# The output projection of a hybrid layer by seven half-size products, and the order in which its weight places are freed

## The reference

```python
mixed = jax.nn.sigmoid(gate_a) * attn_branch + jax.nn.sigmoid(gate_s) * ssm_branch
x = x + mixed @ w_out[i]                      # 256x1024 by 1024x1024, float32
x = x + moe_swiglu(rmsnorm(x, g_ffn[i]), w_router[i], ...)   # top 4 of 32 experts
x = x + sigmoid(rmsnorm(x) @ w_ple_gate) * rmsnorm(p[i] @ w_ple_proj, g_ple_post)
```

## Time and profile before

| | |
|---|---|
| median of three runs | 1183.19 us (1183.05 to 1185.23) |
| the profiled execution | 1185.14 us, its span 1183.4 us |
| granted TensorE clock, mean | 0.992 of full |
| TensorE busy | 1126.7 us, 95% |
| VectorE, ScalarE, GpSimd busy | 372.6, 172.9, 117.6 us |
| DMA moved | 441.16 MB, mean 373 GB/s |
| TensorE in the chain that ended last | 85% |

### The profile page before, as it was taken

One profiled execution on the slowest core, in us unless ns is written; L12 is line 12 of the kernel. 1 busy time (PEld: TensorE's weight loads), 2 busy tenths in 40 slices (PEclk: granted clock), 3 DMA queues, 4 the chain that ended last, 5 costly groups with the idle time before them and its releaser, 6 DMA issues.

```text
span 1183.4 us, 15750 instructions
## 1 busy us (share of the span) xinstructions
PE 1126.7 (95%) x6562; PEld 504.8 (43%) x6562; DVE 372.6 (31%) x831; ACT 172.9 (15%) x262; POOL 117.6 (10%) x151
## 2 busy tenths in 40 slices
PE   7999999999999999999999999999999998999998
PEld 4588887633333333333323333333333333333344
DVE  6547853342222223222222222232222232222222
ACT  2262010510000000000211111111111111111121
POOL 2995650100000000000000000000000000000000
PEclk9999999999999999999979999999999999999999
DMA  9932348699999999999999999999999999999980
GB/s 304 346 116 72 142 165 323 231 415 416 420 430 433 428 432 434 426 433 434 425 394 417 432 434 431 426 435 432 426 436 433 425 435 433 426 435 425 426 347 36
DMA packets 38950, 441.16 MB, mean 373 GB/s; under 512 B 9604, under 2 KB 10176, under 8 KB 22400
## 3 DMA queue, kind: packets, MB, share of 16 engines
q1 hardware_dynamic: 35760, 436.75, 87.9%
q0 software_dynamic: 752, 2.36, 0.6%
q10 hardware_dynamic: 2400, 1.49, 0.4%
HBM read 439.54 MB, written 1.05 MB: 372 GB/s over the span
## 4 chain that ended last, share of the span: by engine, by line
PE 85%; DVE 6%; DMA 6%; ACT 2%; issue 1%; SPq 0%; DVEq 0%
PE bank L1568 35%; PE bank L1624 18%; PE bank L1258 7%; DMA ring<-in_w_up_dram 6%; PE bank L1642 5%; PE bank L1273 3%; PE bank L1463 2%; PE bank L1746 2%; PE bank L1418 2%; PE bank L1606 2%; DVE arena L1098 2%; DVE arena L1102 2%; DVE arena L1096 2%; PE bank L1429 2%; ACT arena L729 1%
## 5 line engine op out<-in xcount | busy, mean ns | idle before, releaser
L1568 PE MATMUL bank<-ring,arena 128*64 128x512 f32 x2048 | 450.7, 597 | 3.5 <-DMA ring<-in_w_up_dram 3.5
L1568 PEld LDWEIGHTS bank<-ring,arena 128*64 128x64 f32 x2048 | 144.2, 137 | 304.4 <-issue 298.1
L1624 PE MATMUL bank<-ring,arena 128*64 128x512 f32 x1024 | 228.5, 599 | 15.8 <-ACT arena L729 14.7
L1120 DVE TENSOR_TENSOR arena<-arena,bank 128x512 f32<-128x512 f32 x128 | 79.8, 682 | 294.8 <-PE bank L1642 294.6
L1624 PEld LDWEIGHTS bank<-ring,arena 128*64 128x64 f32 x1024 | 72.2, 137 | 151.4 <-issue 134.3
L1094 DVE TENSOR_SCALAR arena<-bank 128x512 f32<-128x512 f32 x32 | 22.1, 691 | 344.7 <-PE bank L1568 344.7
L727 ACT ACTIVATE arena<-arena 128x512 f32<-128x512 f32 x32 | 20.2, 630 | 466.3 <-DVE arena L1094 466.3
L1258 PE MATMUL bank<-arena,ring 128*128 128x256 f32 x384 | 86.4, 382 | 0.0
L1258 PEld LDWEIGHTS bank<-arena,ring 128*128 128x128 f32 x384 | 71.8, 190 | 12.7 <-issue 3.5
L1642 PE MATMUL bank<-arena 64*128 64x512 f32 x256 | 68.9, 624 | 0.0
L1542 PEld LDWEIGHTS bank<-arena 128*128 128x128 bf16 x1488 | 45.1, 98 | 25.2 <-issue 25.2
(11 more groups left out here) (250 smaller groups left out, 736.9 us busy)
## 6 DMA issues: line engine op xcount, KB each, us to landing
ring<-in_w_up_dram SPq DMA_DIRECT2D x45, 4096.0 KB, 24.7
ring<-in_w_down_dram SPq DMA_DIRECT2D x27, 4096.0 KB, 27.6
ring<-in_w_up_dram SPq DMA_DIRECT2D x36, 2048.0 KB, 23.5
ring<-in_w_down_dram SPq DMA_DIRECT2D x9, 2048.0 KB, 13.0
ring<-in_w_in_dram SPq DMA_DIRECT2D x7, 2048.0 KB, 16.2
ring<-in_w_glu_dram SPq DMA_DIRECT2D x2, 2048.0 KB, 8.2
ring<-in_w_out_dram SPq DMA_DIRECT2D x2, 2048.0 KB, 7.7
ring<-in_w_up_dram SPq DMA_DIRECT2D x4, 1024.0 KB, 32.4
```

The source lines that it names most:

```text
L1120: dve.tensor_tensor(part, part, bank[at][:, :], ALU.add).then_inc(m["sc_add"], 1)
L1568: last = pe.matmul(bank[UG + w][HALF * h:HALF * (h + 1), :].rearrange("p (m j) -> p m j", j=4), XS[:, k, :], columns[:, h, :, :], start=Fa ...
L1624: last = pe.matmul(bank[YB][HALF * c:HALF * (c + 1), :], ACTT[:, j, HALF * h:HALF * (h + 1)], piece[:, j, 512 * c:512 * (c + 1)], start=(h ...
```

## The change

The matrices are split in halves of the inner dimension and of both outer ones: for tokens early/late block t, inner half j, column half c. Four full products become seven products of four steps each. Sums of the right-hand quarters (`W_SUM`) are made by GpSimd, sums of the left-hand quarters (`M_SUM`) by VectorE. outa and outc accumulate several products in one bank, and VectorE adds the bank to a quarter of X2 after each (`prod_full`, `prod_read`). The seventh product is out3 and out4, in quarters, over columns 0 to 511 of block 1 (they were 512 to 1023).

```diff
+        H2T = area(A_X, DT, SEQ)
+        OUT_W = [[ring[:, PLACE * at:PLACE * (at + 1)].rearrange("p (j a n) -> p j a n", j=2, a=4)[:, j] for j in range(2)]
+                 for at in (6, 7)]
+        W_SUM = [area(A_Q, 4, 512), area(A_Q + 2048, 4, 512), OUT_W[1][0], area(A_BT, 4, 512)]
+        M_SUM = [area(A_GATE + 2048 + at, 4, P) for at in (0, 512, 1536, 1024)]
...
-        LAST = FIRST + (E - 1 - FIRST) // PERIOD * PERIOD
+        LAST = FIRST + 8 * PERIOD
...
+            return FIRST <= n <= LAST and spot(n, c) < PLACES - 1
+
+        HALVES = {(E - 2, 3): "late_0", (E - 1, 3): "late_1", (E - 1, 5): "late_2"}
...
-            for i in range(PLACES):
+            for i in (0, 1, 2, 3, 4, 5, 6, 8, 7):
                 at = spot(0, i)
-                if at in held:
+                if at == TURN["out", 0][0]:
+                    wait_full(sp, "outb")
+                    sp.wait_ge(S["w_sum"], 4)
+                elif at == TURN["out", 1][0]:
+                    wait_full(sp, "outa")
+                elif at in held:
                     wait_full(sp, held[at])
                 elif at == PLACES - 1:
-                    wait_full(sp, "lg1")
+                    sp.wait_ge(S["prod_full"], 3)
+                    sp.wait_ge(S["w_sum"], 4)
                 load_rows(at, expert_source(i // PER_EXPERT, i % PER_EXPERT))
...
-                pool.dma_start(BDOWN[rows, :], b_down[0, :, 512 * (g % 2):512 * (g % 2 + 1)]).then_inc(S["down_bias_in"], 16)
-            pool.dma_start(GPOST, g_ple_post[0:1, :].broadcast_to([P, D])).then_inc(S["post_in"], 16)
-            pool.wait_ge(S["mixed_set"], DT)
...
+            pool.tensor_tensor(W_SUM[0], OUT_W[1][0], OUT_W[0][0], ALU.subtract).then_inc(S["w_sum"], 1)
+            pool.wait_ge(S["w_sum"], 1)
+            pool.tensor_tensor(W_SUM[1], OUT_W[1][1], W_SUM[0], ALU.subtract).then_inc(S["w_sum"], 1)
+            pool.tensor_tensor(W_SUM[2], OUT_W[1][1], OUT_W[1][0], ALU.subtract).then_inc(S["w_sum"], 1)
+            pool.wait_ge(S["w_sum"], 3)
+            pool.tensor_tensor(W_SUM[3], OUT_W[0][1], W_SUM[1], ALU.subtract).then_inc(S["w_sum"], 1)
...
+            wait_full(pool, "lg1")
+            pool.dma_start(WPP, w_ple_proj[0].rearrange("(k p) n -> p k n", p=P)).then_inc(S["ple_in"], 16)
...
+            pool.dma_start(PIN, p[0, 0].rearrange("(t p) n -> p t n", p=P)).then_inc(S["ple_in"], 16)
...
+            pool.dma_start(GPOST, g_ple_post[0:1, :].broadcast_to([P, D])).then_inc(S["post_in"], 16)
...
-            act.dma_start(WPP, w_ple_proj[0].rearrange("(k p) n -> p k n", p=P)).then_inc(S["ple_in"], 16)
-            act.dma_start(PIN, p[0, 0].rearrange("(t p) n -> p t n", p=P)).then_inc(S["ple_in"], 16)
...
-
-            def squared(t, job, cols, to):
-                released(act, job)
+            act.activation(TABLE, ident[:, 0:1], ACT.Sqrt)
+
+            def squared(t, cols, to):
                 act.activation(JUNK[:, cols], X2[:, t, cols], ACT.Square,
                                accum_out=SSQ[:, to:to + 1]).then_inc(S["x2_sq"], 1)
 
...
-            released(act, "out0")
-            squared(0, "out1", slice(0, D), 2)
+            released(act, "outb")
+            squared(0, slice(0, 512), 4)
+            released(act, "outc")
+            squared(0, slice(512, D), 2)
             normal(0)
+            wait_full(act, "outc")
             cast(0, 0)
-            squared(1, "out2", slice(0, 512), 3)
+            act.wait_ge(S["prod_read"], 4)
+            squared(1, slice(512, D), 3)
+            released(act, "out3")
+            squared(1, slice(0, 256), 6)
             cast(0, 1)
-            squared(1, "out3", slice(512, 768), 6)
             cast(0, 2)
-            squared(1, "out4", slice(768, D), 7)
+            released(act, "out4")
+            squared(1, slice(256, 512), 7)
             normal(1)
             cast(1, 0)
...
+            early = [GATE[:, 0:4, P * t:P * (t + 1)] for t in range(TB)]
+            late = [GATE[:, 4:DT, P * t:P * (t + 1)] for t in range(TB)]
+            dve.tensor_tensor(M_SUM[0], early[1], late[1], ALU.add).then_inc(S["m_sum"], 1)
+            dve.wait_ge(S["m_sum"], 1)
+            dve.tensor_tensor(M_SUM[1], M_SUM[0], early[0], ALU.subtract).then_inc(S["m_sum"], 1)
+            dve.tensor_tensor(M_SUM[2], early[0], early[1], ALU.subtract).then_inc(S["m_sum"], 1)
+            dve.wait_ge(S["m_sum"], 2)
+            dve.tensor_tensor(M_SUM[3], late[0], M_SUM[1], ALU.subtract).then_inc(S["m_sum"], 1)
...
+            def add_product(t, c, job, full_by=None):
+
+                if full_by is None:
+                    wait_full(dve, job)
+                else:
+                    dve.wait_ge(S["prod_full"], full_by)
+                part = X2[:, t, 512 * c:512 * (c + 1)]
+                return dve.tensor_tensor(part, part, ps(job)[:, :], ALU.add)
+
+            add_product(0, 0, "outa", 1).then_inc(S["prod_read"], 1)
+            dve.wait_ge(S["prod_read"], 1)
+            release(add_product(0, 0, "outb"), "outb")
+            add_product(1, 1, "outc", 2).then_inc(S["prod_read"], 1)
+            add_product(0, 1, "outa", 3).then_inc(S["prod_read"], 1)
+            dve.wait_ge(S["prod_read"], 3)
+            release(add_product(0, 1, "outc"), "outc")
             dve.wait_ge(S["router_in"], 16 * 3)
             dve.tensor_tensor(WR, WR, spread(GROUT, E), ALU.mult).then_inc(S["router_set"], 1)
             dve.wait_ge(S["x2_sq"], 1)
-            mean_plus_eps(SSQ[:, 2:3], D).then_inc(S["x2_ms"], 1)
+            ts(SSQ[:, 4:5], SSQ[:, 4:5], D * EPS, None, ALU.add)
+            dve.wait_ge(S["x2_sq"], 2)
+            dve.tensor_scalar(SSQ[:, 2:3], SSQ[:, 2:3], SSQ[:, 4:5], 1.0 / D, ALU.add, ALU.mult).then_inc(S["x2_ms"], 1)
             dve.wait_ge(S["x2_root"], 1)
             dve.reciprocal(RSTD[:, 2:3], RSTD[:, 2:3]).then_inc(S["x2_normal"], 1)
-            add_output("out2", 1, slice(0, 512))
+            add_product(1, 1, "outa").then_inc(S["prod_read"], 1)
+            release(add_product(1, 0, "outa"), "outa")
             turned("xt0", 0, 0, 4)
             turned("xt1", 0, 4, 4)
-            add_output("out3", 1, slice(512, 768))
-            dve.wait_ge(S["x2_sq"], 3)
+            released(dve, "outa")
+            add_output("out3", 1, slice(0, 256))
+            dve.wait_ge(S["x2_sq"], 4)
             ts(SSQ[:, 6:7], SSQ[:, 6:7], SSQ[:, 3:4], D * EPS, ALU.add, ALU.add)
             dve.wait_ge(S["x2_normal"], 1)
             choose(0)
-            turned("xt2", 1, 0, 4)
-            turned("xt3", 1, 4, 2)
+            turned("xt2", 1, 4, 4)
+            turned("xt3", 1, 0, 2)
             ranked(0).then_inc(S["sel_first_set"], 1)
-            add_output("out4", 1, slice(768, D))
-            turned("xt4", 1, 6, 2)
-            dve.wait_ge(S["x2_sq"], 4)
+            add_output("out4", 1, slice(256, 512))
+            turned("xt4", 1, 2, 2)
+            dve.wait_ge(S["x2_sq"], 5)
             dve.tensor_scalar(SSQ[:, 3:4], SSQ[:, 7:8], SSQ[:, 6:7], 1.0 / D, ALU.add, ALU.mult).then_inc(S["x2_ms"], 1)
             dve.wait_ge(S["x2_root"], 2)
...
+            def product(job, of, w, ks=range(4), start=False, stop=True, cols=slice(0, 512)):
+
+                b = ps(job)[:, 0:cols.stop - cols.start]
                 for k in ks:
-                    last = pe.matmul(b[:, 0:SEQ], GATE[:, k, P:2 * P], weight(("out", 1), DT)[:, k, cols],
-                                     start=(k == 0), stop=(k == DT - 1))
-                if ks[-1] == DT - 1:
-                    done(last, job)
+                    last = pe.matmul(b, of[:, k, :], w[:, k, cols], start=start and k == 0, stop=stop and k == 3,
+                                     skip_group_check=True)
+                return last
+
+            def quarter(j, t):
+                return GATE[:, 4 * j:4 * (j + 1), P * t:P * (t + 1)]
...
-            output(0)
-            output(1)
-            output(2)
-            released(pe, "out0")
-            released(pe, "out1")
+            take("outa")
+            arrive(("out", 0))
+            pe.wait_ge(S["mixed_set"], 4)
+            product("outa", quarter(0, 0), OUT_W[0][0], start=True).then_inc(S["prod_full"], 1)
+            take("outb")
+            pe.wait_ge(S["mixed_set"], DT)
+            done(product("outb", quarter(1, 0), OUT_W[0][1], start=True), "outb")
+            take("outc")
+            pe.wait_ge(S["w_sum"], 2)
+            pe.wait_ge(S["m_sum"], 2)
+            product("outc", M_SUM[0], W_SUM[0], start=True).then_inc(S["prod_full"], 1)
+            pe.wait_ge(S["prod_read"], 1)
+            product("outa", M_SUM[1], W_SUM[1]).then_inc(S["prod_full"], 1)
+            pe.wait_ge(S["prod_read"], 2)
+            pe.wait_ge(S["m_sum"], 4)
+            arrive(("out", 1))
+            done(product("outc", M_SUM[3], OUT_W[1][1]), "outc")
+            pe.wait_ge(S["prod_read"], 3)
+            pe.wait_ge(S["w_sum"], 4)
+            done(product("outa", M_SUM[2], W_SUM[2]), "outa")
```

(24 more changed lines are left out.)

52 lines of the change are left out of this document (21 added, 31 removed).

## The result

| | before | this |
|---|---|---|
| median, seven runs each | 1183.27 us (1183.05 to 1185.23) | 1188.07 us (1183.12 to 1189.18) |
| the profiled execution, its span | 1185.14, 1183.4 us | 1189.18, 1187.4 us |
| granted TensorE clock, mean | 0.992 | 0.991 |

The ratio is 1.0032 (1.0018 to 1.0047): slower by 0.3%, where 5.2 us less had been forecast. One of the seven executions, 1183.12 us, was as fast as the kernel before; its mean granted clock was 0.994, that of the other six 0.989 to 0.993. The page first: columns as in the earlier trace rows.

The account below looks back on a forecast made before the run. Bound by the matrix engine up to the hole at 604 to 620, by DMA to expert 27, by both behind it. First expert 3.1 us earlier plus late experts 2.1 made 5.2 us less: 1178.0 us, range 1175.2 to 1181.9.

Parts of the forecast that it names:

- DMA idles from 214 to 218 now ... so these 6.3 MB fill holes: Before the first expert: places 6, 8, 7 reload at 203.9, 210.7, 217.6, filling idle DMA; stream leads by 4.5 us.
- the moved loads: Projection, p, down bias and post gain, 2.1 MB on GpSimd's queue at 227 to 236: could cost 4.9 us; none taken.
- The choice of the first block is ready at about 223.3, so rk0 isn't held: Router, first token block: experts chosen at about 223.3, before out4's third step ends at 224.1, so the rank product doesn't wait.
- The rule weighed: VectorE reading two tiles beside GpSimd blocks fully: last tile mixed at 199.2, not 198.9; wanted at 200.4, so the sum stays.
- The late singles: Experts 28 and 29 load single pieces, LAST 27: waits of 1.1 and 0.59 us go; 1.7 to 2.5, taken as 2.1.
- The freed places: Places 6, 7 and 8 reloaded earlier: stream leads by 4.5 us; neither loss nor gain counted in the sum.
- The stretch behind expert 12: Clock and DMA hole at 604 to 620: adjusts the stream to the matrix engine, so a lost lead costs nothing.
- The output projection: From 196.99: seven half-size products, 3.43 us less; three full blocks end at 217.6, first expert starts 3.1 us earlier.
- The sums: GpSimd's four at 4.3 to 5.1 us each, ended by 189.5 to 192.7; VectorE's four end at 201.8; all in time.
- The first one, the stream that takes the earlier start back: DMA continuous to expert 27, so the 3.1 us become waits at experts 26 and 27: 1181.1 us; chance 0.15.
- The slower ones: Another clock hole behind expert 29, 1184.9 us, chance 0.04; GpSimd's and VectorE's sums holding each other, 1184.1 us, chance 0.02.

Follow-up runs that it names:

- a_early: Changed kernel with the five small router and gain loads moved from ScalarE's queue to SyncE's, behind place 3's load; 1187.36 us, ratio 1.0021 to the kernel before.
- a_waitlate: Changed kernel with VectorE's wait for the router loads and its multiplication moved behind the copy of xt1; 1183.55 us, ratio 1.0007 to the kernel before.
- a_oldorder: Changed kernel with reloads of places 6, 7 and 8 held as long as in the kernel before; 1187.22 us, ratio 1.0027 to the kernel before.
- a_early_hold: Changed kernel with the five small loads early and GpSimd's second subtraction held until the first choice; 1181.60 us, ratio 0.9982 to the kernel before.
- a_early_ge: The mended kernel: changed kernel with the small loads early and the choice as one comparison with the fourth largest logit; 1180.39 us, ratio 0.9975.
- b_singles: Kernel before with only LAST at 27, so experts 28 and 29 load single pieces; 1183.89 us, ratio 1.0003.
- a_mend_old: Mended kernel (early small loads, shorter choice) with reloads of places 6 to 8 held as in the kernel before; 1183.68 us, ratio 1.0002 to the kernel before.
- a_mend_pairs: Mended kernel (early small loads, shorter choice) with the old loop limits, pairs up to expert 29; 1178.46 us, ratio 0.9960 to the kernel before.
- a_hold: Changed kernel with only GpSimd's second subtraction held until the first choice, small loads still late; 1191.17 us, ratio 1.0064 to the kernel before.
- a_pairs: Changed kernel with the old loop limits, pairs up to expert 29; 1187.41 us, ratio 1.0028 to the kernel before.
- a_early_pairs: Changed kernel with the five small loads early and the old loop limits; 1187.05 us, ratio 1.0019 to the kernel before.
- a_busy: Changed kernel with out3's four products run three times to keep TensorE busy in its gap; 1186.52 us, ratio 1.0031 to the kernel before.
- b_early: Kernel before with the five small loads moved to SyncE's queue behind place 3; 1185.00 us, ratio 1.0006.

## Why the prediction was wrong, step by step

- **"DMA idles from 214 to 218 now ... so these 6.3 MB fill holes": the step that failed.** The hole was free, but a load issued at 203.9 doesn't wait for it: place 6 (issued at 204.3) follows the running pieces at once and takes DMA from about 208.5 on, just where before the weights' queue ran dry and five small loads of ScalarE's queue got through. VectorE waits for them ahead of its last additions. The prediction asked what the moved loads cost each other, and never what landed in that stretch. The bias took 21.2 us to land, not 10.9; a stall of 5.3 us on TensorE and, behind it, 3.0 us of low clock came of it. a_early and a_waitlate show the wait, a_oldorder that the freed places make it.
- **"The choice of the first block is ready at about 223.3, so rk0 isn't held": failed too, hidden by the first.** The time was right (the comparison starts at 223.43 in a_early, and in a_early_hold the choice is ready at 223.30), the duration not: VectorE's comparison of two tiles met GpSimd's subtraction and took 1.99 us for 0.19. The rule weighed (the Trainium skill, "SBUF — State Buffer", Summary: rules for kernel authors) says just this. The prediction used it for the sums only, where it did no harm, and not for this pair, one of which has only 32 columns. a_early_hold and a_early_ge take the pair apart and get 5.8 and 7.0 us in the median.
- **The late singles, 2.1 us of the sum: wrong.** In the kernel before they measure 1.0003 (0.9994 to 1.0012), and 1.9 us the other way in the mended one. The waits move on to later pieces: expert 29 still has one of 0.93 us in b_singles and of 0.91 in a_early_ge. Why pairs are better in the mended kernel stays open. They move 441 GB/s there at 1045 to 1060 and singles 427, but the kernel before, with pairs, moves 430.
- **The freed places, "no loss" and no gain: mis-sized,** 3.3 us once the start is mended. The stretch behind expert 12 doesn't adjust a late stream: in a_mend_old DMA is busy 0.99 of 604 to 620 and 1.00 of 618 to 624, so it never gets ahead and rests. In a_early_ge it rests a little (0.93, and 0.81 at 612 to 618), as a stream does that has got ahead (argued from the DMA share alone). The first late wait is at 895.77 in a_mend_old, at 978.84 in a_early_ge.
- **The output projection: right.** Six blocks without a gap, 197.26 to 218.02 (20.76 us; forecast 197.0 to 217.6), first additions in time, first up product at 232.3 in a_early_hold (forecast 232.4).
- **The sums: right in the main.** On GpSimd and VectorE, the timeline of after:

```profile
172.64 4.53 POOL L561 TENSOR_TENSOR ring<-ring 128x2048 f32<-128x2048 f32 x1
177.24 4.59 POOL L563 TENSOR_TENSOR ring<-ring 128x2048 f32<-128x2048 f32 x1
```
```profile
177.49 4.62 DVE L1002 TENSOR_TENSOR arena<-arena 128x256 f32<-128x256 f32 x1
...
192.32 0.43 DVE L1002 TENSOR_TENSOR arena<-arena 128x256 f32<-128x256 f32 x1
...
198.95 0.42 DVE L1002 TENSOR_TENSOR arena<-arena 128x256 f32<-128x256 f32 x1
```

GpSimd's take 4.5 to 4.7 us each (4.3 had been taken, 5.1 was the bound) and end at 191.2, not 189.5; and the gate products beside them shut out for up to 4.63 us where they take 0.42. Two columns are through by 191.4, the rest catch up, and the last tile is mixed at 199.4 (by the rule 199.2, wanted at 200.4).
- **The rivals.** None named a wait for a small load. The first one, the stream that takes the earlier start back, is what a_mend_old shows, with the old order of reloads. The slower ones had 0.06 together; the case that came would have stood among them if the list of queued loads had been read for this stretch as it was for the ring.
- **Luck.** a_mend_pairs, at 1178.46, lies beside the forecast's 1178.0, but not by its sum: it has no single pieces, which held 2.1 of the 5.2 us, and it has a shorter choice and the freed places, which the sum had at nothing.

**What stays open.** Why the clock falls: it follows a new gap of TensorE in after, a_hold, a_pairs, a_early, a_oldorder and a_early_pairs (1.06 to 5.27 us), but a_waitlate has a gap of 1.00 us and a_busy one of 0.98 with no fall right behind, and b_early shows 0.50 at 236 to 238 without a new one. It doesn't fall alike in every execution. a_early took 1182.42 us at a mean granted clock of 0.996, 1183.63 to 1185.40 at 0.993, and 1185.83 to 1188.36 at 0.989 to 0.991. Where in an execution it fell is known for the profiled ones alone, so how the change's loss in the median divides between the wait for the bias, the collision and the clock is not.

## What to carry to other kernels

A transfer that is freed early starts early: it doesn't wait for the hole of DMA that it is meant to fill. So list every transfer, on every queue, that lands between its new start and the hole, and who waits for it; then look at what is queued behind that wait. A wait for something small belongs right ahead of its use, not where the engine was once idle. And when engines close up, go through the pairs that now run at once, tiny operations included: a second stall may lie hidden behind the first, so a mended wait that brings nothing is no proof against it.

## What was new about the hardware

- A VectorE operation on two tiles of the main memory that met a running GpSimd tensor operation ended with it, however short it is: 0.42 us became 4.63, 0.19 became 2.00. A comparison with one tile and one number per token (128x64) was held in the same way, 0.73 to 1.24 us for 0.26.
- The bias, one of five loads in 1744 packets (92 bytes each on average), landed in 21.2 us beside back-to-back 2 MB loads, and in 10.9 and 10.0 where their queue ran dry from 209 on. The Trainium skill ("DMA: Bandwidth & Descriptors", Queues, rings and completion order) says that a DMA engine takes turns between queues packet by packet. The trace agrees: 269 packets of each queue from 204 to 213, and 942 small ones in one microsecond alone.
- After a gap of only 1.06 us in a stretch of small products (a_early) the granted clock stood at 0.50 for several us; after one of 1.00 us (a_waitlate) it stayed at 1.00.
